# All x stores issued by ScalarE one step behind the split, and the gate block's products in the order 2, 1, 5, 3, 6, 7, 4

## What is computed

```python
def reference(x, norm_w, w_in, sinks, conv_w, conv_b, w_out, rel_bias, final_norm_w):
    for l in range(DEPTH):
        hn = rmsnorm(x, norm_w[l])
        proj = jnp.einsum('bsd,de->bse', hn, w_in[l])
        q, k, v, g_attn, h, c_gate, b_gate, g_conv = jnp.split(proj, SPLIT_POINTS, axis=-1)
        attn = swa_sink_attention(q, k, v, sinks[l], rel_bias)
        conv = short_gated_conv(h, c_gate, b_gate, conv_w[l], conv_b[l])
        mixed = jnp.concatenate([attn * jax.nn.silu(g_attn),
                                 conv * jax.nn.silu(g_conv)], axis=-1)
        x = x + jnp.einsum('bse,ed->bsd', mixed, w_out[l])
    return rmsnorm(x, final_norm_w)
```

## Time and profile before

| | us |
|---|---|
| median of 3 runs | 1344.7 (1343.59 to 1345.12) |
| the profiled execution | 1342.97 |
| its span | 1341.2 |
| TensorE busy in it | 1326.5 |
| VectorE, ScalarE, GpSimd busy | 919.1, 538.7, 91.5 |

### The profile page before, as it was taken

How to read it: one execution, slowest core, us unless ns; L and a number is a source line. 1 busy time by engine, 2 the same in 40 slices (tenths; PEclk the granted TensorE clock), 3 DMA queues, 4 the chain that set the end, 5 groups by cost and what they waited for, 6 DMA issues and landing times.

```text
span 1341.2 us, 16590 instructions
## 1 busy us (share of the span) xinstructions
PE 1326.5 (99%) x6038; PEld 1098.0 (82%) x6038; DVE 919.1 (69%) x1144; ACT 538.7 (40%) x940; POOL 91.5 (7%) x155
## 2 busy tenths in 40 slices
PE   9999999999999999999999999999999999999997
PEld 7788888888888888888888888878888888888886
DVE  7898886323578459975589745998438896656376
ACT  7745532222233433434334343343423444321455
POOL 1222321000000000000000000000000222100001
PEclk9999999999999999999999999999999999999999
DMA  9878995988898999869998799878898978899778
GB/s 358 316 274 306 410 369 152 313 309 317 298 295 242 299 298 272 260 200 307 310 292 247 236 287 300 261 251 248 296 332 295 336 261 280 288 314 358 281 255 310
DMA packets 205200, 390.02 MB, mean 291 GB/s; under 512 B 79008, under 2 KB 128192, under 8 KB 183488
## 3 DMA queue, kind: packets, MB, share of 16 engines
q1 hardware_dynamic: 185520, 322.09, 73.3%
q0 software_dynamic: 18304, 62.92, 12.8%
q10 hardware_dynamic: 1296, 3.96, 0.8%
HBM read 294.18 MB, written 98.93 MB: 293 GB/s over the span
## 4 chain that ended last, share of the span: by engine, by line
PE 92%; DVE 4%; issue 2%; ACT 1%; DMA 1%; SPq 0%; POOL 0%; POOLq 0%; DVEq 0%; ACTq 0%
PE banks L2063 89%; PE banks L2092 1%; PE banks L2104 1%; DVE w_ring L1378 1%; PE banks L2113 1%; PE banks L2114 1%; DMA z<-in_x_t_dram 1%; DVE raw L1475 0%; DVE e L1541 0%; DVE z L1447 0%; DVE x_main L1391 0%; DVE raw L1481 0%; ACT x_main L1029 0%; DVE e L1562 0%; PE banks L1988 0%
## 5 line engine op out<-in xcount | busy, mean ns | idle before, releaser
L2063 PE MATMUL banks<-x_main,w_ring 128*128 128x512 f32 x2352 | 550.4, 391 | 3.0 <-DVE x_main L1391 2.8
L2063 PEld LDWEIGHTS banks<-x_main,w_ring 128*128 128x128 f32 x2352 | 437.8, 188 | 94.1 <-issue 3.9
L998 ACT ACTIVATE w_ring<-raw 128x1024 fp32r<-128x1024 f32 x223 | 235.5, 1056 | 554.6 <-PE banks L2063 541.0
L1378 DVE TENSOR_TENSOR w_ring<-raw,w_ring 128x1024 fp32r<-128x1024 f32 x223 | 272.7, 1223 | 215.3 <-ACT w_ring L998 213.8
L2063 PE MATMUL banks<-x_far,w_ring 128*128 128x512 f32 x1680 | 393.5, 391 | 0.1
L2063 PEld LDWEIGHTS banks<-x_far,w_ring 128*128 128x128 f32 x1680 | 313.0, 188 | 64.8 <-DVE e L1541 0.5
L2063 PE MATMUL banks<-w_ring,x_main 128*128 128x512 f32 (+1 forms) x1020 | 231.0, 387 | 0.3 <-DVE e L1541 0.3
L2063 PEld LDWEIGHTS banks<-w_ring,x_main 128*128 128x128 f32 x1020 | 189.9, 188 | 39.6 <-DVE e L1541 0.7
L511 POOL DMA_DIRECT2D x_park<-x_main x104 | 56.1, 539 | 1012.0 <-DVE x_main L1391 1011.9
L1029 ACT ACTIVATE x_main<-z 128x512 fp32r<-128x512 f32 x104 | 64.9, 624 | 123.8 <-issue 102.6
L1391 DVE TENSOR_TENSOR x_main<-z,x_main 128x512 fp32r<-128x512 f32 x104 | 71.2, 686 | 38.0 <-ACT x_main L1029 37.6
(11 more groups left out here) (166 smaller groups left out, 861.3 us busy)
## 6 DMA issues: line engine op xcount, KB each, us to landing
x_far<-x_park SPq DMA_DIRECT2D x84, 1024.0 KB, 7.1
x_main<-x_park SPq DMA_DIRECT2D x84, 1024.0 KB, 7.2
x_park<-x_main POOLq DMA_DIRECT2D x104, 512.0 KB, 5.7
raw<-in_w_in_dram SPq DMA_DIRECT2D x130, 256.0 KB, 5.3
raw<-in_w_out_dram SPq DMA_DIRECT2D x32, 512.0 KB, 5.7
raw<-in_w_in_dram SPq DMA_DIRECT2D x31, 512.0 KB, 12.6
q_cur<-qkv_park SPq DMA_DIRECT2D x64, 128.0 KB, 5.3
z<-mix_park SPq DMA_DIRECT2D x16, 512.0 KB, 8.3
```

The costliest lines, as they stand in the source:

```text
L998: act.activation(w_ring[:, n % NW, :, 0, :], raw[:, c, k:k + 2, :], ACT.Copy).then_inc(w_hi_ready, 1)
L1378: dve.tensor_tensor(w_ring[:, n % NW, :, 1, :], raw[:, c, k:k + 2, :], w_ring[:, n % NW, :, 0, :], ALU.subtract).then_inc(w_lo_ready, 1)
L2063: op = pe.matmul(bank, left, right, start=(first and i == 0), stop=(kt == HK - 1 and i == 2), skip_group_check=goes_on)
```

## The change

The third product of the gate block becomes 5 (columns' sum s1 times t1) instead of 3 (which needs s1, s2 and s4, and x from place_1). Tables, counts and the copies out of PSUM follow: product 5 is copied by ScalarE, and 7 is added from the copies. All stores of x_main leave GpSimd for ScalarE: each is issued one step after x_lo was written, in quarter 1. The eight parked halves all go through two stages in e and are stored at steps 10 to 18 by GpSimd. w_lo goes behind pt_lo also when a block's first product meets a unit (late_w).

```diff
-ORDER = [(2, 1, 3, 6, 7, 5, 4)] + [(2, 1, 6, 7, 5, 3, 4)] * 5 + [(1, 2, 3, 6, 7, 5, 4), (2, 1, 6, 7, 5, 3, 4)]
+ORDER = [(2, 1, 5, 3, 6, 7, 4)] + [(2, 1, 6, 7, 5, 3, 4)] * 5 + [(1, 2, 3, 6, 7, 5, 4), (2, 1, 6, 7, 5, 3, 4)]
...
-COPIED = [(o[0], 3, 7) if b in ON_CHIP else (o[0], 6, 7) for b, o in enumerate(ORDER)]
-ADDED = [(o[1], 6, 5, 4) if b in ON_CHIP else (o[1], 5, 3, 4) for b, o in enumerate(ORDER)]
+COPIED = [(2, 5, 3, 7) if b == GATES else (o[0], 3, 7) if b == OUT0 else (o[0], 6, 7) for b, o in enumerate(ORDER)]
+ADDED = [(1, 6, 7, 4) if b == GATES else (o[1], 6, 5, 4) if b == OUT0 else (o[1], 5, 3, 4) for b, o in enumerate(ORDER)]
...
-            if p == 3 and b not in ON_CHIP:
+            if p == 3 and b != OUT0:
...
-S1_AT = {(5, 0): 0, (7, 0): 1, (7, 2): 2, (8, 0): 3}
-S24_AT = {(6, 1): 0, (7, 1): 1, (7, 3): 2, (8, 2): 3}
+S1_AT = {(5, 0): 0, (7, 0): 1, (7, 2): 2, (8, 3): 3}
+S24_AT = {(8, 1): 0, (9, 1): 1, (10, 1): 2, (11, 1): 3}
...
-B21_AT = {(10, 3): 0, (13, 3): 1, (18, 3): 2, (19, 3): 3}
-PARK_AT = {(11, 1): 0, (11, 3): 1, (15, 1): 2, (16, 1): 3, (21, 1): 4, (21, 3): 5, (22, 1): 6, (22, 3): 7}
-STAGED = 4
+B21_AT = {(9, 3): 0, (12, 3): 1, (13, 3): 2, (14, 3): 3}
+PARK_AT = {(10, 1): 0, (11, 1): 1, (13, 1): 2, (14, 1): 3, (15, 1): 4, (16, 1): 5, (17, 1): 6, (18, 1): 7}
...
-        park_stage = [e[:, i, 2 * j:2 * j + 2, :] for i in (1, 3) for j in range(2)]
+        park_stage = [e[:, 3, 2 * (j % 2):2 * (j % 2) + 2, :] for j in range(HK)]
-        park_stored = sem("park_stored")
+        park_stored = [sem(f"park_stored{i}") for i in range(2)]
...
+                    if b == QKV and (c, j // QP) == (1, 0):
+                        sp.wait_ge(s2_ready, j + 1)
...
-                        elif p == 5:
+                        elif p == (6 if b == GATES else 5):
...
-                if j < STAGED:
-                    if j == 2:
-                        pool.wait_ge(park_stored, 16 * 2)
-                    pool.wait_ge(park_lo_ready, j + 1)
-                    pool.dma_start(x_park[0, j // 2, :, j % 2, :], park_stage[j].rearrange("p a c -> p (a c)")
-                                   ).then_inc(park_stored, 16)
-                    return
-                if j == STAGED:
-                    pool.wait_ge(park_stored, 16 * STAGED)
-                pool.wait_ge(park_hi_ready, j + 1)
-                pool.dma_start(x_park[0, j // 2, :, j % 2, 0:N], z[:, 1, j, :]).then_inc(park_stored, 16)
                 pool.wait_ge(park_lo_ready, j + 1)
-                pool.dma_start(x_park[0, j // 2, :, j % 2, N:], z[:, 0, HK + j, :]).then_inc(park_stored, 16)
+                pool.dma_start(x_park[0, j // 2, :, j % 2, :], park_stage[j].rearrange("p a c -> p (a c)")
+                               ).then_inc(park_stored[j % 2], 16)
...
-                    for l in X_LO_AT.get((n, quarter), ()):
-                        if not is_parted(l // 2):
-                            store_x(pool, l // 2, l % 2)
-                    l = 2 * n + 3 + quarter
-                    if n >= 0 and quarter < 2 and X_TABLED <= l < 2 * LEN:
-                        store_x(pool, l // 2, l % 2)
...
-                for l in (2 * n + 3, 2 * n + 4):
-                    if l < 2 * STEPS and l // (2 * LEN) == OUT0:
-                        store_x(pool, l // 2, l % 2)
...
-                if j < STAGED:
-                    act.wait_ge(x1_turned, KT)
-                    act.activation(park_stage[j][:, 0, :].bitcast(F32R), z[:, 0, HK + j, :], ACT.Copy
-                                   ).then_inc(park_hi_ready, 1)
-                    return
-                act.wait_ge(x_lo_ready, x_index(at(GATES, 5, j // 2), j % 2) + 1)
-                act.activation(z[:, 1, j, :].bitcast(F32R), z[:, 0, HK + j, :], ACT.Copy).then_inc(park_hi_ready, 1)
+                act.wait_ge(x1_turned, KT)
+                if j > 1:
+                    act.wait_ge(park_stored[j % 2], 16 * (j // 2))
+                act.activation(park_stage[j][:, 0, :].bitcast(F32R), z[:, 0, HK + j, :], ACT.Copy).then_inc(park_hi_ready, 1)
 
...
+                    elif to == 1:
+                        act.wait_ge(x1_turned, KT)
...
-                            act.wait_ge(park_stored, 16 * STAGED)
+                            act.wait_ge(gate_ready, 2)
...
+                    for l in X_LO_AT.get((n - 1, quarter), ()):
+                        if not is_parted(l // 2):
+                            store_x(act, l // 2, l % 2)
+                    if quarter == 1:
+                        for l in (2 * n + 1, 2 * n + 2):
+                            if X_TABLED <= l < 2 * LEN or l // (2 * LEN) == OUT0:
+                                store_x(act, l // 2, l % 2)
...
+                elif p == 7:
+                    dve.wait_ge(copy_ready, copy_count(b, 7, t))
+                    dve.tensor_tensor(e1, e1, e3, ALU.add).then_inc(sum_ready, 1)
...
-                    late_w = CONV0 <= b < OUT0 and i == 6 and unit_at(n, 2)[1] == 10 and unit_at(n, 2)[0] < UNITS
+                    late_w = CONV0 <= b < OUT0 and i in (0, 6) and unit_at(n, 2)[1] == 10 and unit_at(n, 2)[0] < UNITS
...
-                        if quarter == 1 and 12 <= n < 12 + QP:
-                            s3(GATES, n - 12)
+                        if quarter == 1 and 15 <= n < 15 + QP:
+                            s3(GATES, n - 15)
...
-                        late = 1 if b == GATES else 0
+                        late = 4 if b == GATES else 0
...
-                        late = 2 if b == GATES else 0
+                        late = 5 if b == GATES else 0
...
-                        late = 4 if b == GATES else 0
+                        late = 6 if b == GATES else 0
```

More of the change, by code:

```diff
@@ L98, in copy_count @@
 def copy_count(b, p, t):
-    return sum(3 * w for w in WIDE[:b]) + COPIED[b].index(p) * WIDE[b] + t + 1
+    return sum(len(c) * w for c, w in zip(COPIED[:b], WIDE)) + COPIED[b].index(p) * WIDE[b] + t + 1
 def sum_count(b, p, t):
@@ L147, in _banks @@
             loose = []
-            if not (p in (1, 6) or (p == 5 and b not in ON_CHIP)):
+            if not (p in (1, 6) or (p == 5 and b != OUT0)):
                 loose = mine
@@ L761, in _ @@
                     if b == GATES:
-                        if (i, q, quarter) == (4, 3, 1):
+                        if (i, q, quarter) == (5, 1, 1):
                             store_gate(0, 0, 0)
-                        if i == 4 and q >= 2 and quarter in (0, 2):
+                        if i == 5 and q >= 2 and quarter in (0, 2):
                             load_more(q - 2, quarter // 2)
@@ L1124, in tanh_gate @@
             def tanh_gate(i, half):
-                to = (1, 0, 0, 0)[i]
-                p = (ORDER[GATES][1], 5, 5, 4)[i]
+                to = (3, 0, 0, 0)[i]
+                p = (1, 7, 6, 4)[i]
                 act.wait_ge(sum_ready, sum_count(GATES, p, 3))
@@ L1131, in tanh_gate @@
                 else:
-                    act.wait_ge(park_stored, 16 * 2)
+                    act.wait_ge(park_stored[0], 16 * HK // 2)
+                    act.wait_ge(park_stored[1], 16 * HK // 2)
                 if i > 1:
@@ L1305, in _ @@
                     if b == GATES:
-                        if (i, q) == (4, 1) and quarter in (1, 3):
+                        if (i, q) == (4, 3) and quarter in (1, 3):
                             tanh_gate(0, quarter // 2)
@@ L1544, in sums @@
                     dve.tensor_tensor(e2, e2, ps, ALU.add).then_inc(sum_ready, 1)
-                elif p == 5 and b in ON_CHIP:
+                elif p == 7:
+                    dve.wait_ge(copy_ready, copy_count(b, 7, t))
+                    dve.tensor_tensor(e1, e1, e3, ALU.add).then_inc(sum_ready, 1)
+                elif p == 5 and b == OUT0:
                     dve.wait_ge(copy_ready, copy_count(b, 7, t))
@@ L1558, in sums @@
                 else:
-                    dve.wait_ge(sum_ready, sum_count(b, 5, t))
+                    dve.wait_ge(sum_ready, sum_count(b, 7 if b == GATES else 5, t))
                     if b == OUT1:
@@ L1872, in _ @@
                     if b == GATES:
-                        if (i, q) == (4, 2) and quarter in (1, 3):
+                        if (i, q) == (5, 0) and quarter in (1, 3):
                             silu_gate(0, quarter // 2)
@@ L2029, in wait_bank @@
                 was = BANK_BEFORE[b, p, t]
-                if b == GATES and p == 3:
+                if b == GATES and p == 5:
                     pe.wait_ge(x1_placed, HK)
@@ L2052, in product @@
                 w, a = w_ring[:, n % NW, kt % 2, :, :], x_halves(n)[kt % 2]
-                goes_on = p in (6, 7) or (p == 3 and b not in ON_CHIP)
+                goes_on = p in (6, 7) or (p == 3 and b != OUT0)
                 first = kt == 0 and not goes_on
```

19 lines of the change are left out of this document (7 added, 12 removed).

## The result

The changed kernel takes 1350.15 us (median, 1348.22 to 1351.41), beside 1344.35 of the kernel before in the same runs: slower by 0.4%, ratio 1.0040 (1.0029 to 1.0052), or 5.8 us. I had forecast 1344.8 and a range up to 1349.0. Both of the gains came; what outweighed them are losses that my sum had at nothing.

What follows compares the result with a forecast made beforehand. TensorE, busy 1326.5 of 1341.2 us, was taken as the bound, so only its idle time counts. -2.8 + 4.0 - 1.1 = +0.1 gave 1344.8 us, range 1340.6 to 1349.0.

Steps and rivals of the forecast that it cites:

- Removed at step 8: Start of step 8: product 5 needs no s2 or s4, so TensorE's waits for x_lo, 2.5 and 0.3, go: -2.8 us.
- Step 141: In step 141, w_lo moved behind pt_lo ends TensorE's wait of 1.2 us for pt_lo: -1.1 us.
- The early round trip: Steps 4 to 7: later stores, landing in 7.0 us each, make x_hi(15) and so TensorE late: +4.0 us.
- What would show it: Expected trace signs, among them stores at 36.7, x_hi(13) near 43.7, x_hi(15) near 50.8, TensorE waiting about 4 us near 50.
- The steady loop: Settled steps: stores on ScalarE land within the 6.5 us before their slot is wanted; cost 0, at most +1.5 in OUT0.
- the third rival: Over six dense steps, 10 us landings make the ring the bound: up to +18 us, 2 to 3 at 8.5; chance 0.10.
- The new order's own costs in the dense stretch: Product 5 for 3, ScalarE's four extra copies and parked stores in steps 10 to 18 were taken to cost nothing.
- tanh_gate(0), costed at nothing: Parked halves go out in steps 10 to 18, the last formerly made in step 22, so reloads come earlier; no cost.
- the second rival: ScalarE's store issues take 1.87 us each, as SyncE's did, delaying activations and x_hi: +3.5, 1348.2 us; chance 0.17.
- The forecast's own range: Main forecast with landing of 6 to 8.1 us (+2.0 to +6.2) and OUT0's bound: 1342.8 to 1347.5 us; chance 0.45.

Runs made afterwards that it cites:

- the fastest kernel: Changed kernel with halves 8 to 18 stored by GpSimd, the others by ScalarE in the step that makes them, tanh_gate(0) one step later: 1340.28 us.

## Why the prediction was wrong, point by point

**Removed at step 8, -2.8: right.** The row at 64.66 has no break, and in the kernel with all stores on GpSimd at once TensorE starts its 501st matmul at 104.4 us, 3.2 before the kernel before does. No wait of TensorE is put down to s2 or s4 in steps 8 to 11. **Step 141, -1.1: right,** measured 1.2.

**The early round trip, +4.0: right in mechanism, too large by the trace.** Issue at 37.54 (forecast 36.7), x_hi(13) at 44.02 (43.7), x_hi(15) at 50.04 (50.8), t1 at 52.45, TensorE's transposes 3 us later than the earlier trace rows. DMA issues of the changed kernel at 37.5 to 38 us and at 43 to 44.5 us:

```profile
x_park<-x_main ACTq DMA_DIRECT2D x2, 512.0 KB, 7.8
...
x_park<-x_main ACTq DMA_DIRECT2D x1, 512.0 KB, 5.9
```

The 7.8 is the median of a pair. The store that x_hi(13) waited for is the first of it and took 6.4, so the two links of the chain were 6.4 and 5.9 and not 7.0 each. Nine tenths of a microsecond of the lateness were there before: the square of the earlier trace rows at 36.64 began at 37.53, and TensorE was already 0.9 behind at 13 us, ahead of all ring stores (the profiled executions of the other kernels are 0.0 to 0.9 behind there). What the chain itself added is the other 2.3 of x_hi(15)'s 3.2, and TensorE's waits near 45 and 53 grew by 2.2, where "What would show it" has about 4. Undoing this part gave 3.5.

The Trainium skill says on the page "DMA: Bandwidth & Descriptors", section "Queues, rings and completion order", that a DMA engine takes turns between its queues. With the prediction's estimate of 3.2 us by that page, this term would have been 0, if taking turns had let a store pass SyncE's backlog. The store at 37.54 had no older store on its queue and took 6.4 all the same, so the trace doesn't bear that inference out; whether the engines took turns, these rows don't show.

**The steady loop, "so I take 0": this is the step that failed.** I compared the time that the loop leaves, 6.5, with medians, 7.2 and 6.9, and wrote "0.4 to 0.7 late in a step" and several us of slack. The runs show a cost of 2.0 (GpSimd, a step late against at once) to 5.3 (ScalarE, 1346.67 against 1341.34). The 5.3 holds the waits at 117, 123, 191 and, in most executions, 1080. Three things were wrong.

First, the issue came at 1.0 to 1.4 us of the step (steps with issues at 95.93 and 101.94), so the second of them left 5.5 and not 6.5.

Second, "in the dense ones the median is 7.2" is true of 125 to 150 us alone. The densest part follows it, and the trace of the kernel before shows it, in its DMA issues at 130 to 165 us:

```profile
x_park<-x_main POOLq DMA_DIRECT2D x13, 512.0 KB, 9.8
```

From 145 to 168 us nine stores of that kernel have a median of 10.3 and a longest of 12.7. So "only the tail of them lies above 8.5", which gave the third rival (the ring becomes the bound) its 0.10, was a misreading. The rival's own prices, 2 to 3 at 8.5 and up to 18 at 10, have what came between them.

Third, the loop feels its long landings and not their median: at 101.94 a store took 9.96, and the ring passes the excess on, since the next store stands behind the delayed x_hi.

**The new order's own costs in the dense stretch, "costs nothing": wrong too.** The time from the start of TensorE's 501st matmul to that of its 851st, by the profile of each kernel:

| order | ring stores | us |
|---|---|---|
| old | at once or in their own step (2 kernels) | 79.4, 79.4 |
| old | a step late | 82.7 |
| new | at once or in their own step (6 kernels) | 80.7 to 83.0 |
| new | a step late (5 kernels) | 84.5 to 87.2 |

These are single executions, and the same gate block gave 87.2 once and 84.5 another time. Within one order the late kernels still lie above all the others, from either engine. A step of lateness costs 3 to 4 us here with either order, and the new order costs 1.3 to 3.6 even where no store is late, which takes back about as much as step 8 gained. Of that, the wait of 0.2 to 0.6 for a sum near 132 to 137 is in all kernels with the new order and in none with the old, and tanh_gate(0) is another part. The rest is not assigned.

**tanh_gate(0), costed at nothing.** I had written only that the parked halves go out sooner and the reloads with them. But tanh_gate(0) writes the tiles in which they are staged. The last is issued in step 18 (131.59), tanh_gate stood in step 19, and the landing came at 139.4; ScalarE was blocked for 7.67. It is worth 1.1 to 2.1 in the three pairs of kernels that differ in it (1350.15 and 1348.52, 1343.66 and 1341.60, 1341.34 and 1340.28; only the last two were timed beside each other).

The steps by what was measured: from the fastest kernel back to the changed one, tanh_gate +1.1, the stores from 19 on a step behind +5.3, the early ones +3.5: 1340.28 + 9.9 = 1350.2. This is one run less the next, so it closes by itself and proves no term.

**ScalarE's issues held up like SyncE's** (the second rival): no. An issue took 0.33 in the median, also at 37.54, beside the same traffic as SyncE's slow ones of the earlier trace rows. Of the 104, eleven took over 0.5, and two over 1: 1.21 at 51.75 and 1.44 at 102.37. So full DMA engines alone don't make an issue slow.

**Two things in the arithmetic.** The forecast's own range has 1347.5 as its upper end; 1344.7 - 3.9 + 6.2 + 1.5 is 1348.5. And the forecast missed by 5.4 although the +4.0 was too large: the two errors lie on opposite sides.

What stays open: with ScalarE late and the early stores on GpSimd, the waits that can be read one by one are 0.30, 1.56, 1.53 and 1.51 - 0.32 = 4.6 of the 5.3, and the profiled executions of the two kernels are 4.1 apart. Open is also whether late stores cost less from GpSimd (1345.67) than from ScalarE (1346.67), since the two were not timed beside each other; why in the new order stores in time are cheaper from ScalarE (1340.28) than from GpSimd (1341.60), which were; and what the new order costs between 107 and 187 us beyond the waits named.

## What to carry to other kernels

A store out of a ring is part of the loop that refills the ring: moving its issue later by a step can move the landing into the path, however free the issuing engine is. Hold the time that the loop leaves against the longest landings of the densest stretch (10 to 13 us here), not against a median of a stretch that leaves them out (7.2), and ask whether the next store is behind the delayed writer. When an order of work changes, go through each buffer that a moved operation writes and look at who must have landed from it; a single wait of 7.7 us on a landing, in a list that runs in order, cost 1 to 2 us here. Where the engine's list was ahead of its work, it mattered little which engine issues (0.6 us with the old order, not clear of noise, and 1.3 with the new); where a wait in the list was itself on the path, it cost 2.0.
